# A one-core decoder trunk: six stages a layer with the down projection amid the next stage's gate and up, and 28 groups of seven products in place of 16

## The chip, the cores and the metric

One core of a Trainium2 chip runs the whole program. The metric is the device time of one execution in microseconds (us).

## The reference

Two layers over 256 tokens of 2048 features. The first mixes tokens with a causal pooling, the second with latent attention; each then has the same feed-forward part, which is what the change touches:

```python
def swiglu(h, w_gate, w_up, w_down):
    return (jax.nn.silu(h @ w_gate) * (h @ w_up)) @ w_down

x = x + swiglu(rms_norm(x, ffn_norm[l]), w_gate[l], w_up[l], w_down[l])   # for each of the two layers
```

`w_gate` and `w_up` are 2048 x 5632, `w_down` is 5632 x 2048, all float32.

## The kernel before

**Numbers.** Every float32 factor is split in two rounded parts, hi and lo, and a product is three matmuls: hi x hi, hi x lo, lo x hi. Weights stream from memory into `raw` in chunks of 128 x 1024 elements. ScalarE writes `w_hi` (its `split`), VectorE writes `w_lo = raw - w_hi` (its `split`), into one of four slots (`SPLIT_SLOTS`). TensorE reads both. Chunk n + 4 can be split only when TensorE has ended chunk n (`chunks_used`), and TensorE starts a chunk when its lo part is there (`lo_ready`).

**Plain chunks.** The 5632 features of the hidden layer are 44 tiles of 128. For a plain tile four chunks (two of gate, two of up, half of the 2048 inputs each) are each eight pairs of matmuls: `w_hi` against hi and lo of the activations side by side (512 columns), `w_lo` against hi (256 columns), L634 and L635.

**Groups of seven products.** Two tiles at a time can be computed by a scheme of Strassen's kind: the inputs (two halves) and the tokens (two halves) make a 2 x 2 block product, done with seven half-size products P1 to P7 in place of eight. Each product is two chunks of four times three matmuls of 256 columns (L804, L806, L807). The four weight quarters W11, W12, W22, W21 lie in eight slots of `raw`. Some products need sums of quarters, made in place: first `W11 += W12` (for P5), then `W11 += W22` (P6), `W12 += W22` (P7), `W21 += W11` (P4). The first two are VectorE's (`add_quarter`, L1674), the last two are DMAs that accumulate within SBUF, issued by GpSimd (L2214). The products go P1, P5, P6, P2, P7, P3, P4. They add up in PSUM, and between them intermediate sums are copied out: ScalarE's `part_copy` (L1239) takes P1, then P5, then P1 + P6; TensorE's P2 waits for the copy of P5, P7 for that of P6 (`part_copied`). VectorE adds, gates and multiplies (L1712, L1718), and TensorE turns four blocks back with transposes (L819).

**Order.** A layer's 44 tiles go in three passes of 16, 14 and 14 tiles, with 2, 3 and 3 groups. `up_order` mixes each pass's group chunks evenly with its plain chunks, with plain chunks alone at the head and seven at the end. After a pass's gate and up comes its down projection, 16 output tiles of 14 or 16 products each from two chunks, added into the residual `x` by VectorE (`into_x`, L1791, L1792). Each engine runs its own instruction list in order. Loads are issued by SyncE in an order worked out from when slots come free (`up_loads`): plain chunks have three slots of their own, a quarter's slot is reloaded once its last product is split, and W11's once the fourth sum has landed.

Of the kernel before, what the change touches and what calls it, by code (L numbers as in the profile page):

```python
# [44 lines left out]
P = 128  # L45
# [29 lines left out]
PLAIN_SLOTS = 3  # L75
# [31 lines left out]
PRODUCTS = ("P1", "P5", "P6", "P2", "P7", "P3", "P4")  # L107
# [4 lines left out]
def up_order(q):  # L112

    groups = PASS_GROUPS[q]
    seven = [("S", g, r, c) for g in range(groups) for r in PRODUCTS for c in range(2)]
    plain = [("P", p, c) for p in range(PASS_TILES[q] - 2 * groups) for c in range(4)]
    lead, tail = PASS_LEAD[q], PASS_TAIL
    order, mixed, done = plain[:lead], plain[lead:len(plain) - tail], 0
    for k, s in enumerate(seven):
        order.append(s)  # L120
        upto = (k + 1) * len(mixed) // len(seven)
        order += mixed[done:upto]
        done = upto
    return order + plain[len(plain) - tail:]


UP_ORDER = [up_order(q) for q in range(PASSES)]
PLAIN_TILES = [t - 2 * g for t, g in zip(PASS_TILES, PASS_GROUPS)]
PLAIN_BEFORE = [sum(PLAIN_TILES[:q]) for q in range(PASSES + 1)]
GROUPS_BEFORE = [sum(PASS_GROUPS[:q]) for q in range(PASSES + 1)]  # L130
UPS = [f"up{q}" for q in range(PASSES)]
DOWNS = [f"down{q}" for q in range(PASSES)]
# [23 lines left out]
def up_pass(n):  # L156

    for q in range(PASSES):
        if CHUNK[UPS[q]] <= n < CHUNK[DOWNS[q]]:
            return q  # L160
    return None


def up_step(n):

    q = up_pass(n)
    return None if q is None else UP_ORDER[q][n - CHUNK[UPS[q]]]


PLAIN_AT = [CHUNK[UPS[q]] + k for q in range(PASSES) for k, s in enumerate(UP_ORDER[q]) if s[0] == "P"]  # L170
PLAIN_NO = {n: k for k, n in enumerate(PLAIN_AT)}
GROUP_AT = {(GROUPS_BEFORE[q] + s[1], s[2], s[3]): CHUNK[UPS[q]] + k
            for q in range(PASSES) for k, s in enumerate(UP_ORDER[q]) if s[0] == "S"}


def raw_slot(n):
# [4 lines left out]
    if s[0] == "P":  # L181
        return RING_SLOTS + PLAIN_NO[n] % PLAIN_SLOTS
# [8 lines left out]
def freed_by(g, w, c):  # L191

    return GROUP_AT[g, {"W11": "P2", "W12": "P7", "W22": "P3", "W21": "P4"}[w], c]
# [7 lines left out]
def up_loads(q):  # L201

    loads = []
    for k, s in enumerate(UP_ORDER[q]):
        n = CHUNK[UPS[q]] + k
        if s[0] == "P":
            before = PLAIN_NO[n] - PLAIN_SLOTS
            free = PLAIN_AT[before] if before >= 0 else 0
            loads.append((max(free, CHUNK[UPS[q]] - 1), n, ("chunk", n)))
    for g in range(GROUPS_BEFORE[q], GROUPS_BEFORE[q + 1]):  # L210
        for w in QUARTERS:
            for c in range(2):
                free = freed_by(g - 1, w, c) + (3 if w == "W11" else 0) if g > GROUPS_BEFORE[q] else 0
                if free == 0 and q % LAYER_PASSES == 0 and w in ("W22", "W21"):
                    free = CHUNK[UPS[q]] + MIX_STEPS + SPLIT_SLOTS
                loads.append((max(free, wanted_by(g, w, c) - 14, CHUNK[UPS[q]] - 1), wanted_by(g, w, c),
                              ("quarter", g, w, c)))
# [3 lines left out]
UP_LOADS = [up_loads(q) for q in range(PASSES)]  # L221


def load_numbers():

    numbers, count, order = {}, [0] * (RING_SLOTS + PLAIN_SLOTS), []
    for n in range(CHUNK["end"]):
        q = up_pass(n)
        if q is None:
            order.append(("chunk", n))  # L230
        elif n == CHUNK[UPS[q]]:
            order += UP_LOADS[q]
# [39 lines left out]
def trunk(nc, xT, positions, consts, bands, gains, pool_first, pool_w, w_kv_a, w_k_pe, w_q_a, w_kv_k, w_kv_v, w_q_nope, w_q_pe,  # L272
          w_o, w_plain, w_group, w_down_first, w_down_rest, w_last, final_gain, out):
    with ExitStack() as ctx:
# [8 lines left out]
        raw = sb("raw", [P, RING_SLOTS + PLAIN_SLOTS, TILES * P])  # L283
# [31 lines left out]
        act = at("act", [P, max(PASS_TILES), 2 * SEQ], F32R, region_at + 32 * KB)  # L315
# [33 lines left out]
        angle, turns = part[:, 0, :], part[:, 1, :]  # L349
# [40 lines left out]
        landed = [sem(f"landed{s}") for s in range(RING_SLOTS + PLAIN_SLOTS)]  # L390
# [1993 lines left out]
```

## Time and profile before

| | us |
|---|---|
| median of 3 runs | 1746.03 (1745.45 to 1746.16) |
| the profiled execution, its own time | 1746.25 |
| its span, first to last instruction | 1744.4 |
| TensorE busy | 1736.1 |
| VectorE busy | 1339.1 |
| ScalarE busy | 986.0 |
| GpSimd busy | 168.2 |

The profile is of one execution. The span leaves out 1.85 us of the execution's own time. An engine's busy time is the time in which at least one of its instructions ran; TensorE's matmuls overlap, so a mean duration of one is longer than the time from one to the next.

### The profile page before, as it was taken

The numbers are of one execution on the slowest core, as the hardware profiler recorded it, in microseconds if no ns is written. First come the engines' busy times: TensorE is split into PE (matmuls) and PEld (weight loads), VectorE is DVE, ScalarE is ACT, GpSimd is POOL, SyncE is SP. The second block draws the span as 40 slices with busy tenths as digits, with TensorE's granted clock in tenths as the row PEclk, the third lists the DMA queues.
The fourth block names the chain that finished last, engine by engine and source line by source line (L and its number), as shares of the span: only waits on it lengthen the run. The fifth ranks groups of instructions, "written<-read, shape, count | busy, mean of one in ns | idle before, by whom it ended". The sixth has DMA issues, their size and how long they took to land. (4 is left out here: it accounts for less than half of the span.)

```text
span 1744.4 us, 29460 instructions
## 1 busy us (share of the span) xinstructions
PE 1736.1 (100%) x11142; PEld 1575.2 (90%) x11142; DVE 1339.1 (77%) x1772; ACT 986.0 (57%) x1336; POOL 168.2 (10%) x196
## 2 busy tenths in 40 slices
PE   9999999999999999999999999999999999999998
PEld 6899988999889999889999888998899998899987
DVE  5898766788667886788997779876678866788665
ACT  6666543566435665466775456664356653466543
POOL 2100000000000000324112420000000000000000
PEclk9999999999999999999999999999999999999999
DMA  6678665786767876665445457867568866688762
GB/s 227 216 231 245 234 192 190 238 252 170 248 200 203 251 232 216 200 199 159 150 139 170 156 165 244 242 186 252 196 191 246 247 214 203 200 252 243 227 214 91
DMA packets 103937, 363.24 MB, mean 208 GB/s; under 512 B 11664, under 2 KB 13072, under 8 KB 103696
## 3 DMA queue, kind: packets, MB, share of 16 engines
q1 hardware_dynamic: 94320, 327.03, 54.5%
q0 software_dynamic: 9216, 33.56, 11.2%
q8 instruction: 74, 1.21, 0.3%
q10 hardware_dynamic: 288, 1.11, 0.2%
q14 instruction: 39, 0.32, 0.1%
HBM read 326.01 MB, written 2.10 MB: 188 GB/s over the span
## 5 line engine op out<-in xcount | busy, mean ns | idle before, releaser
L1594 DVE TENSOR_TENSOR w_lo<-raw,w_hi 128x1024 fp32r<-128x1024 f32 (+1 forms) x720 | 858.0, 1201 | 257.3 <-ACT w_hi L1148 251.4
L1148 ACT ACTIVATE w_hi<-raw 128x1024 fp32r<-128x1024 f32 (+1 forms) x721 | 741.4, 1035 | 473.9 <-PE ps L635 390.2
L634 PE MATMUL ps<-xg,w_hi 128*128 128x512 f32 x1856 | 653.2, 392 | 0.8 <-DVE w_lo L1594 0.3
L635 PE MATMUL ps<-xg,w_lo 128*128 128x256 f32 x1856 | 522.9, 282 | 0.0
L634 PE MATMUL ps<-act,w_hi 128*128 128x512 f32 x1352 | 469.2, 390 | 0.0
L634 PEld LDWEIGHTS ps<-xg,w_hi 128*128 128x128 f32 x1856 | 348.4, 188 | 72.2 <-DVE w_lo L1594 2.3
L635 PE MATMUL ps<-act,w_lo 128*128 128x256 f32 x1352 | 381.2, 282 | 0.0
L635 PEld LDWEIGHTS ps<-xg,w_lo 128*128 128x128 f32 x1856 | 350.4, 189 | 0.0
L634 PEld LDWEIGHTS ps<-act,w_hi 128*128 128x128 f32 x1352 | 253.8, 188 | 53.1
L635 PEld LDWEIGHTS ps<-act,w_lo 128*128 128x128 f32 x1352 | 255.5, 189 | 0.0
L2214 POOL DMA_DIRECT2D raw<-raw x64 | 55.3, 865 | 1128.5 <-DVE raw L1674 977.6
L806 PE MATMUL ps<-w_lo,mix_hi_lo 128*128 128x256 f32 x512 | 144.1, 281 | 0.0
L807 PE MATMUL ps<-w_hi,mix_hi_lo 128*128 128x256 f32 x512 | 143.7, 281 | 0.0
L804 PE MATMUL ps<-w_hi,mix_hi_lo 128*128 128x256 f32 x512 | 143.7, 281 | 0.0
L806 PE MATMUL ps<-w_lo,xg 128*128 128x256 f32 x384 | 108.1, 282 | 0.0
L804 PE MATMUL ps<-w_hi,xg 128*128 128x256 f32 x384 | 107.9, 281 | 0.0
L807 PE MATMUL ps<-w_hi,xg 128*128 128x256 f32 x384 | 107.8, 281 | 0.0
L804 PEld LDWEIGHTS ps<-w_hi,mix_hi_lo 128*128 128x128 f32 x512 | 96.4, 188 | 2.7
L807 PEld LDWEIGHTS ps<-w_hi,mix_hi_lo 128*128 128x128 f32 x512 | 96.5, 189 | 0.0
L806 PEld LDWEIGHTS ps<-w_lo,mix_hi_lo 128*128 128x128 f32 x512 | 96.4, 188 | 0.0
L634 PE MATMUL ps<-heads,w_hi 128*128 128x512 f32 x256 | 89.1, 391 | 0.0
L1674 DVE TENSOR_TENSOR raw<-raw 128x1024 f32<-128x1024 f32 x64 | 78.0, 1219 | 0.0
(232 smaller groups left out, 1961.8 us busy)
## 6 DMA issues: line engine op xcount, KB each, us to landing
raw<-w_plain SPq DMA_DIRECT2D x224, 512.0 KB, 4.6
raw<-w_group SPq DMA_DIRECT2D x128, 512.0 KB, 5.8
raw<-w_down_rest SPq DMA_DIRECT2D x120, 448.0 KB, 4.1
raw<-raw POOLq DMA_DIRECT2D x64, 512.0 KB, 5.7
raw<-w_down_first SPq DMA_DIRECT2D x64, 512.0 KB, 4.4
raw<-w_o SPq DMA_DIRECT2D x32, 512.0 KB, 3.5
raw<-w_q_a SPq DMA_DIRECT2D x8, 512.0 KB, 4.2
raw<-w_kv_a SPq DMA_DIRECT2D x8, 512.0 KB, 4.3
```

Source lines behind the costliest of these rows:

```text
L634: pe.matmul(ps[:, bank, :], w_hi[:, s, j * P:(j + 1) * P], moving, start=start, stop=False)
L635: return pe.matmul(ps[:, bank, 0:SEQ], w_lo[:, s, j * P:(j + 1) * P], moving[:, 0:SEQ], start=False, stop=stop)
L804: pe.matmul(dst, x_hi, wh, start=(kt == 0 and r in ("P1", "P5")), stop=False, skip_group_check=True)
L806: pe.matmul(dst, x_hi, wl, start=False, stop=False, skip_group_check=True)
L807: mm = pe.matmul(dst, x_lo, wh, start=False, stop=(kt == TILES - 1), skip_group_check=True)
L1148: nc.scalar.activation(dst, src, ACT.Copy).then_inc(hi_ready, 1)
L1594: nc.vector.tensor_tensor(lo, src, hi.bitcast(F32), ALU.subtract).then_inc(lo_ready, 1)
L1674: nc.vector.tensor_tensor(raw[:, dst, :], raw[:, dst, :], raw[:, src, :], ALU.add).then_inc(done, 1)
L2214: gp.dma_start(raw[:, quarter_slot(into, c), :], raw[:, quarter_slot(of, c), :], accum_op=ALU.add).then_inc(done, 16)
```

## The change

A layer now has one up list, `UP_ORDER`, of 340 chunks for six stages of 8, 6, 6, 8, 8, 8 tiles with 0, 3, 2, 3, 3, 3 groups: 14 groups a layer, 28 in all, and 16 plain tiles a layer. The down projection of a stage is 16 chunks (D), one for each output tile, of 6 or 8 pairs of matmuls, mixed between the next stage's group and plain chunks; only the last stage's down comes by itself at the end. The D chunks share the plain chunks' three slots. Down results are added to `x` after each D chunk (`down_out_of`). The products go P1, P5, P2, P6, P7, P3, P4. The second sum, `W11 += W22`, is an accumulating DMA too, so GpSimd issues six a group where it issued four. Two of the buffers `part` are doubled by `square` and `root`. The table of angles for the rotary phases is made by VectorE in steps amid the first layer's list.

```diff
-PASSES = 6
-LAYER_PASSES = PASSES // 2
-PASS_TILES = (16, 14, 14, 16, 14, 14)
-PASS_GROUPS = (2, 3, 3, 2, 3, 3)
-PASS_LEAD = (24, 4, 4, 24, 4, 4)
-PASS_TAIL = 7
+LAYERS = 2
+STAGE_TILES = (8, 6, 6, 8, 8, 8)
+STAGE_GROUPS = (0, 3, 2, 3, 3, 3)
+STAGES = len(STAGE_TILES)
+STAGE_PLAIN = tuple(t - 2 * g for t, g in zip(STAGE_TILES, STAGE_GROUPS))
+LAYER_GROUPS, LAYER_PLAIN = sum(STAGE_GROUPS), sum(STAGE_PLAIN)
+HALF = max(STAGE_TILES)
 MIX_STEPS = 18
-FH = PASS_TILES[-1]
+GROUPS_FROM = 20
+SETTLE = 8
+ROPE_AT = tuple(range(40, 92, 4))
+TURN_AFTER = 6
+TAIL = 8
+W11_LAG = 5
+FH = STAGE_TILES[-1]
...
-PRODUCTS = ("P1", "P5", "P6", "P2", "P7", "P3", "P4")
+PRODUCTS = ("P1", "P5", "P2", "P6", "P7", "P3", "P4")
...
+    seven = [[("S", sum(STAGE_GROUPS[:s]) + g, r, c) for g in range(STAGE_GROUPS[s]) for r in PRODUCTS for c in range(2)]
+             for s in range(STAGES)]
+    plain = [[("P", sum(STAGE_PLAIN[:s]) + p, c) for p in range(STAGE_PLAIN[s]) for c in range(4)] for s in range(STAGES)]
+    early = plain[0][GROUPS_FROM:]
+    order = plain[0][:GROUPS_FROM] + evenly(early, seven[1][:len(early)])
+    seven[1] = seven[1][len(early):]
+    for s in range(1, STAGES):
+        down = [("D", s - 1, d) for d in range(DT)]
+        last = plain[s][-TAIL:] if s == STAGES - 1 else []
+        rest = plain[s][:len(plain[s]) - len(last)]
+        first = min(len(rest), SETTLE // 3)
+        order += evenly(seven[s][:SETTLE - first], rest[:first])
+        order += evenly(seven[s][SETTLE - first:], evenly(down, rest[first:])) + last
+    return order
+
+
+UP_ORDER = up_order()
+UPS = [f"up{layer}" for layer in range(LAYERS)]
...
-    return GROUP_AT[g, {"W11": "P2", "W12": "P7", "W22": "P3", "W21": "P4"}[w], c]
+    return GROUP_AT[g, {"W11": "P6", "W12": "P7", "W22": "P3", "W21": "P4"}[w], c]
...
+        def part_of(g, at):
+
+            if g % 2 and at in (0, 2):
+                return (square if at == 0 else root)[:, :]
+            return part[:, at, :]
...
+            def down_chunk(layer, k):
+
+                _, s, d = UP_ORDER[k]
+                n, before = CHUNK[UPS[layer]] + k, downs_before(layer, k)
+                pe.wait_ge(lo_ready, made(n))
+                if d == 0:
+                    pe.wait_ge(group_ready, layer * LAYER_GROUPS + sum(STAGE_GROUPS[:s + 1]))
+                    pe.wait_ge(act_ready, layer * LAYER_PLAIN + sum(STAGE_PLAIN[:s + 1]))
+                if before >= 2:
+                    pe.wait_ge(down_out, before - 1)
+                for j in range(STAGE_TILES[s]):
+                    mm = product3(n, j, down_bank(layer, before), act[:, act_slot(s, j), :], j == 0, j == STAGE_TILES[s] - 1)
+                mm.then_inc(chunks_used, 1)
+
...
+                turned_before = g if at == 1 else g - 1
+                if turned_before >= 1:
+                    sc.wait_ge(part_turned, turned_before)
+                nc.scalar.activation(part_of(g, at), src, ACT.Copy).then_inc(part_copied, 1)
...
-                elif step[2] == "P5":
-                    add_quarter(g, "W22", step[3], second_sum)
...
+            def down_out_of(layer, k, d):
+
+                bank, xd = down_bank(layer, downs_before(layer, k)), x[:, d, :]
+                ve.wait_ge(chunks_used, done_at(layer, k))
+                step(nc.vector.tensor_tensor(xd, ps[:, bank, 0:SEQ], xd, ALU.add))
+                nc.vector.tensor_tensor(xd, ps[:, bank, SEQ:], xd, ALU.add).then_inc(down_out, 1)
...
-                        gp.wait_ge(second_sum, 2 * g + c + 1)
+                        gp.wait_ge(landed[quarter_slot("W22", c)], 16 * LOAD_NO["quarter", g, "W22", c])
+                        gp.wait_ge(lo_ready, made(GROUP_AT[g, "P5", c]))
+                        add_quarter("W11", "W22", c, second_sum[c])
+                    for c in range(2):
                         add_quarter("W12", "W22", c, third_sum[c])
                     for c in range(2):
-                        gp.wait_ge(lo_ready, made(GROUP_AT[g, "P2", c]))
+                        gp.wait_ge(lo_ready, made(GROUP_AT[g, "P6", c]))
                         add_quarter("W21", "W11", c, fourth_sum[c])
```

TensorE, in the second group of the first layer's list, before. These are the last matmuls of a plain chunk (L634, L635) and the first three of P2, which waits for the copy of P5:

```order
L634 MATMUL ps<-xg,w_hi 128x512
L635 MATMUL ps<-xg,w_lo 128x256
L804 MATMUL ps<-w_hi,xg 128x256 [waits part_copied,lo_ready]
L806 MATMUL ps<-w_lo,xg 128x256
L807 MATMUL ps<-w_hi,xg 128x256
```

Between P5 and this row stand both chunks of P6 and plain chunks. TensorE, the change, in the fourth group (number 3): the last matmuls of P5's second chunk (L895 to L898, inputs `mix_hi_lo`) and the first of P2 (inputs `xg`):

```order
L895 MATMUL ps<-w_hi,mix_hi_lo 128x256
L897 MATMUL ps<-w_lo,mix_hi_lo 128x256
L898 MATMUL ps<-w_hi,mix_hi_lo 128x256
L895 MATMUL ps<-w_hi,xg 128x256 [waits part_copied,lo_ready]
L897 MATMUL ps<-w_lo,xg 128x256
L898 MATMUL ps<-w_hi,xg 128x256
```

P2, with its wait for the copy, now stands right behind P5. So it is in nine of the layer's 14 groups; in the other five a D or plain chunk is between. P7 stands right behind P6, whose copy it waits for, in four groups (6, 9, 11 and 12), where before P2's two chunks were between.

ScalarE, before, in the second group: the copies (L1239) and the hi splits (L1148) around them, from the first split that needs the second sum on:

```order
L1148 ACTIVATE w_hi<-raw 128x1024 [waits chunks_used,second_sum]
L1148 ACTIVATE w_hi<-raw 128x1024 [waits chunks_used,landed9]
L1148 ACTIVATE w_hi<-raw 128x1024 [waits chunks_used,second_sum]
L1239 ACTIVATE part<-ps 128x256 [waits part_turned,chunks_used]
L1148 ACTIVATE w_hi<-raw 128x1024 [waits chunks_used,landed10]
```

ScalarE, the change, in the second group (number 1, `square` and `root` are its copies' buffers), around the copies of P1 and P5:

```order
L1330 ACTIVATE square<-ps 128x256 [waits chunks_used]
L1238 ACTIVATE w_hi<-raw 128x1024 [waits chunks_used,landed7]
L1238 ACTIVATE w_hi<-raw 128x1024 [waits chunks_used,second_sum0]
L1330 ACTIVATE root<-ps 128x256 [waits chunks_used]
L1238 ACTIVATE w_hi<-raw 128x1024 [waits chunks_used,second_sum1]
```

The split of P6's first chunk, which waits for the second sum's DMA (`second_sum0`), stands ahead of the copy of P5 (the row on `root`). So it is in groups 1 and 11 of each layer, where ten and eleven group chunks follow one another with no D or plain chunk between; in the other groups the copy comes first.

On GpSimd's list the third sums are now issued right behind the second ones (the last lines of the diff), so four accumulating DMAs of a group stand one behind the other in its queue, and two more follow once P6's chunks are split.

## Rows read from the trace of the kernel before

**Rows 1.** The page: span, busy time by engine; DMA queues: packets, MB, share

```profile
span 1744.4 us, 29460 instructions
...
PE 1736.1 (100%) x11142; PEld 1575.2 (90%) x11142; DVE 1339.1 (77%) x1772; ACT 986.0 (57%) x1336; POOL 168.2 (10%) x196
...
q1 hardware_dynamic: 94320, 327.03, 54.5%
q0 software_dynamic: 9216, 33.56, 11.2%
```

**Rows 2.** Groups by line and form: xcount | busy us, mean ns | idle before

```profile
L1148 ACT ACTIVATE w_hi<-raw 128x1024 fp32r<-128x1024 f32 x593 | 624.2, 1058 | 358.6 <-PE ps L635 275.1 <-DMA raw<-w_plain 41.6 <-PE ps L807 32.4
...
L1674 DVE TENSOR_TENSOR raw<-raw 128x1024 f32<-128x1024 f32 x64 | 78.0, 1219 | 0.0
```

**Rows 3.** The chain of waits, of TensorE's weight loads: total us, times, longest

```profile
PEld ps L634 <- DVE w_lo L1594: 2.3, 7, 0.5
```

**Rows 4.** Timeline, TensorE: start us, us; a plain chunk, two group chunks, the next

```profile
372.07 0.39 PE L634 MATMUL ps<-xg,w_hi 128*128 128x512 f32 x1
...
374.86 0.28 PE L804 MATMUL ps<-w_hi,xg 128*128 128x256 f32 x1
...
377.70 0.39 PE L634 MATMUL ps<-xg,w_hi 128*128 128x512 f32 x1
```

**Rows 5.** Timeline, TensorE: eight pairs in a stretch of plain chunks

```profile
79.65 0.39 PE L634 MATMUL ps<-xg,w_hi 128*128 128x512 f32 x1
...
82.42 0.39 PE L634 MATMUL ps<-xg,w_hi 128*128 128x512 f32 x1
```

**Rows 6.** Timeline, TensorE: the four transposes of a group

```profile
156.91 0.60 PE L819 MATMUL ps<-const,part 128*128 128x128 f32 x4
157.27 0.37 PE L804 MATMUL ps<-w_hi,xg 128*128 128x256 f32 x1
157.47 0.28 PE L806 MATMUL ps<-w_lo,xg 128*128 128x256 f32 x1
```

**Rows 7.** Timeline, all engines: a group product ends, ScalarE copies it

```profile
118.51 0.28 PE L807 MATMUL ps<-w_hi,mix_hi_lo 128*128 128x256 f32 x1
118.83 0.39 ACT L1239 ACTIVATE part<-ps 128x256 f32<-128x256 f32 x1 [0.15 <-PE ps L807]
...
118.90 0.51 PE L634 MATMUL ps<-xg,w_hi 128*128 128x512 f32 x1
...
119.24 0.28 PE L635 MATMUL ps<-xg,w_lo 128*128 128x256 f32 x1
```

**Rows 8.** Timeline, ScalarE, then VectorE: end of an up stretch, last plain tile

```profile
218.16 0.60 ACT L1224 ACTIVATE cross<-ps 128x512 f32<-128x512 f32 x1 [1.65 <-PE ps L635]
...
221.22 0.42 ACT L1232 ACTIVATE act<-product 128x256 fp32r<-128x256 f32 x1 [0.49 <-DVE product L1700]
...
221.67 0.42 DVE L1705 TENSOR_TENSOR act<-product,act 128x256 fp32r<-128x256 f32 x1 [0.48 <-ACT act L1232]
```

**Rows 9.** The accumulating DMAs' line: their issue on GpSimd, their landing

```profile
L2214 POOL DMA_DIRECT2D raw<-raw x64: 852/862/1010, 115.4 to 1613.8; - x64
...
DMA to landing us min/median/max: 4.5/5.7/9.4
```

**Rows 10.** Timeline, VectorE: a down tile's two adds between two splits

```profile
481.63 0.42 DVE L1791 TENSOR_TENSOR x<-ps,x 128x256 f32 x1 [0.47 <-PE ps L635]
...
482.50 1.09 DVE L1594 TENSOR_TENSOR w_lo<-raw,w_hi 128x896 fp32r<-128x896 f32 x1
```

**Rows 11.** Timeline, VectorE: four splits one after the other

```profile
164.10 4.63 DVE L1594 TENSOR_TENSOR w_lo<-raw,w_hi 128x1024 fp32r<-128x1024 f32 x4
```

**Rows 12.** Windows of 10 us: PE, PEld, DVE, ACT, POOL busy, clock, DMA share, GB/s

```profile
360.00:370.00 10.00, 10.00 (x72) 9.35 (x71) 9.96 (x12) 6.97 (x12) 1.72 (x2) 1.00 0.82 191
610.00:620.00 10.00, 10.00 (x72) 9.34 (x71) 8.91 (x14) 6.71 (x9) 0.00 (x0) 1.00 1.03 411
160.00:170.00 10.00, 10.00 (x71) 9.35 (x71) 8.78 (x10) 7.23 (x10) 1.72 (x2) 1.00 1.00 226
```

More of the change, by code:

```diff
@@ L127, with evenly @@
[L127 to L132, printed above, removed]
+def evenly(a, b):
+    out, done = [], 0
+    for k, item in enumerate(a):
+        out.append(item)
+        upto = (k + 1) * len(b) // len(a)
+        out += b[done:upto]
+        done = upto
+    return out
@@ L135, in chunk_plan, with stage_of, plain_tile, group_tile @@
+UP_ORDER = up_order()
+UPS = [f"up{layer}" for layer in range(LAYERS)]
+DOWNS = [f"down{layer}" for layer in range(LAYERS)]
+def stage_of(before, k):
+    return next(s for s in range(STAGES) if k < sum(before[:s + 1]))
+def plain_tile(p):
+    s = stage_of(STAGE_PLAIN, p)
+    return s, 2 * STAGE_GROUPS[s] + p - sum(STAGE_PLAIN[:s])
+def group_tile(g):
+    s = stage_of(STAGE_GROUPS, g)
+    return s, 2 * (g - sum(STAGE_GROUPS[:s]))
+def act_slot(s, f):
+    return s % 2 * HALF + f
 def chunk_plan():
@@ L191, in freed_by, with up_loads @@
 def freed_by(g, w, c):
-    return GROUP_AT[g, {"W11": "P2", "W12": "P7", "W22": "P3", "W21": "P4"}[w], c]
+    return GROUP_AT[g, {"W11": "P6", "W12": "P7", "W22": "P3", "W21": "P4"}[w], c]
 def wanted_by(g, w, c):
     return GROUP_AT[g, {"W11": "P1", "W12": "P1", "W22": "P5", "W21": "P2"}[w], c]
[L201 to L210, printed above, removed]
+def up_loads(layer):
+    loads, first = [], CHUNK[UPS[layer]]
+    for k, s in enumerate(UP_ORDER):
+        n = first + k
+        if s[0] != "S":
+            before = STREAM_NO[n] - STREAM_SLOTS
+            free = STREAM_AT[before] if before >= 0 else 0
+            loads.append((max(free, first - 1), n, ("chunk", n)))
+    for g in range(layer * LAYER_GROUPS, (layer + 1) * LAYER_GROUPS):
@@ L211, in up_loads @@
         for w in QUARTERS:
             for c in range(2):
[L213 to L217, printed above, removed]
+                if g > layer * LAYER_GROUPS:
+                    free = freed_by(g - 1, w, c) + (W11_LAG if w == "W11" else 0)
+                elif w in ("W22", "W21"):
+                    free = first + MIX_STEPS + SPLIT_SLOTS
+                else:
+                    free = first - 1
@@ L218, in up_loads @@
+                loads.append((max(free, wanted_by(g, w, c) - 14, first - 1), wanted_by(g, w, c), ("quarter", g, w, c)))
     return [load for _, _, load in sorted(loads, key=lambda x: x[:2])]
-UP_LOADS = [up_loads(q) for q in range(PASSES)]
+UP_LOADS = [up_loads(layer) for layer in range(LAYERS)]
 def load_numbers():
-    numbers, count, order = {}, [0] * (RING_SLOTS + PLAIN_SLOTS), []
+    numbers, count, order = {}, [0] * (RING_SLOTS + STREAM_SLOTS), []
     for n in range(CHUNK["end"]):
-        q = up_pass(n)
-        if q is None:
+        layer = up_layer(n)
+        if layer is None:
@@ L1862, in _ @@
+                n1, t1 = CHUNK[DOWNS[layer]], TILE[DOWNS[layer]]
+                for d in range(DT):
+                    into_x(t1 + d, d, n1 + d + 1)
+                    split(n1 + d + SPLIT_SLOTS)
+                    gained(d, G_ATTN, xg, xg_before + d + 1)
+            ffn(0, 2, DT)
             xk_tiles = iter(range(DT))
```

690 lines of the change are left out of this document (341 added, 349 removed).

## Prediction

> **What bounds the kernel now.** I read the page first. TensorE is busy for 1736.1 of a span of 1744.4 us, VectorE for 1339.1, ScalarE for 986.0 [rows 1]; so TensorE is the bound unless its busy time hides waits. The chain of waits says that it hides hardly any: for a split chunk TensorE waited 2.3 us in all, in seven waits of at most 0.5 [rows 3]. A timeline of TensorE then gives the price of its work. The start of one chunk to the start of the next is 2.79 us for a plain chunk and, over two, 1.42 us for a group chunk [rows 4]; where only plain chunks run, eight pairs take 2.77 [rows 5]. The kernel's time is therefore the sum of these pieces. The windows say how near the others are: between 360 and 370 us VectorE is busy for 9.96 of 10 us while TensorE still never stands, and the DMA share touches 1.00 with and without accumulating DMAs [rows 12].
>
> **What TensorE gains.** Two tiles as plain chunks are 8 x 2.78 (between the two rows) = 22.2 us; as a group 14 x 1.42 = 19.9 us [rows 4, 5]: 2.36 us less. Twelve more groups give 28.3. Each also brings four transposes: from 156.91 to 157.27, and the matmul behind them holds 0.20 where 0.12 is usual, 0.44 us in all [rows 6], 12 times 5.3. Net **-23.0** (-22.1 to -24.0 with the one or the other price of a plain chunk). The down projection has as many pairs as before but for the last quarter of the last layer, where 24 pairs more (8.3 us) stand against six fewer inputs of the closing part: three matmuls of 512 and six of 256 columns each, about 1.4 us apiece, 8.4. I count that as nothing.
>
> **What the new product order costs.** This is the term on which the sign hangs. P2 waits for ScalarE's copy of P5, and P7 for that of P6. Before, at least two group chunks (2.84 us) lay between; now none does in 9 + 4 of a layer's 14 groups, 26 places in all. What such a place costs is seen in a product that ends and is copied: its last matmul starts at 118.51, the copy at 118.83, 0.32 later, and takes 0.39 [rows 7]. From one engine's end to the next one's start is 0.03 (ScalarE's 221.22 + 0.42 to VectorE's 221.67) [rows 8]. TensorE's next matmul would have started 0.12 after the last; so it starts 0.32 + 0.39 + 0.03 - 0.12 = 0.62 late. The first matmul after a stand also holds longer: 118.90 to 119.24, 0.34, against 2.77 / 8 - 0.12 = 0.23 [rows 5, 7]. That is 0.11 more, with rounding 0.74 a place, 26 times **+19.2**. From below: without the last 0.11 and the tail of the copy I would still have 0.48 (12.5 in all). From above: ScalarE may still hold a split (1.06 us [rows 2]) or a gate when the product ends, at most half a microsecond more, 1.2 a place, 31 in all. I take 0.74, since ScalarE is free in rows 7.
>
> **The end of a layer's up list.** Before, the last plain tile was the 14th or 16th input of the first down tile. From the copy of its cross terms to its finished lo part are 221.67 + 0.42 - 218.16 = 3.93 us [rows 8]; 13 pairs at 0.346 are 4.5, so nothing stood. Now it is the eighth input, reached after 7 x 0.346 = 2.42 us. With 0.32 ahead and 0.03 and 0.11 behind, less the 0.12, TensorE stands 0.32 + 3.93 + 0.14 - 2.54 = 1.85 us, in both layers **+3.7** (bounds 3 and 5).
>
> **The second sum as a DMA.** An accumulating DMA lands 5.7 us (4.5 to 9.4) after its issue [rows 9], where VectorE's sum took 1.22 [rows 2]. P6's split can begin only then. The lo part of a chunk is there some 2.6 us after TensorE ends the chunk four ahead: ScalarE's 1.06, VectorE's 1.22 [rows 2] and hops; the DMA of P5's first chunk thus lands at 2.6 + 5.7 = 8.3 from that end. In 12 groups of a layer TensorE has 11 us and more of work up to the ScalarE step that needs it. In groups 1 and 11 it is different, and here the order rows on ScalarE count: the split of P6 stands ahead of the copy of P5, so P2 can start only at 8.3 + 1.06 + 0.39 + 0.1 = 9.9. TensorE gets to P2 in group 1 after five group chunks, 7.1 us, and in group 11 after a plain chunk and four group chunks, 8.45. It stands 2.8 and 1.45, of which 0.74 each is counted above: 2.1 and 0.7 more. In group 11 a second wait follows. Four DMAs stand behind one another, and the last must have landed for P7's second chunk. The accumulating queue took 11.2% of the span for 64 DMAs, 3.05 us each [rows 1]; the last lands near 2.6 + 2 + 4 x 3 = 16.6, and with the split's 2.3 the chunk is ready at 18.9. TensorE is there at 9.9 + 4 x 1.42 + 0.74 + 1.42 = 17.7: 1.2 less rounding, say 0.7. Together 3.5 a layer, **+7.0**. From below: with the shortest landing (4.5) and the loads aside, 4, and nothing if TensorE comes later than I think. From above: with 9.4 in place of 5.7 the two groups lose 3.7 more each, and then the reload of W11, which waits for the fourth sum, is late too: 24 in all.
>
> Here a page would give another sum. The Trainium skill ("DMA: Bandwidth & Descriptors", section "Anatomy of one DMA — SWDGE (gpsimd) path") puts a GpSimd-issued DMA at 2.0 us plus its bytes at 436 GB/s; by that, 512 KB would land in 3.2 us, both waits would all but vanish and my sum would be 7 us lower, 1746. The trace disagrees, 4.5 us at least [rows 9], so I keep the row.
>
> **What should stay hidden.** DMA throughput: a load at full share runs at 411 GB/s, 1.28 us for 512 KB, while with accumulating DMAs in the mix the same full share moves 226 GB/s [rows 12]. A stage with three groups has 48 loads (61 us) and 18 sums (55 us), 116 us under TensorE's 42 x 1.42 + 24 x 2.78 = 126: 92%. It fits on average; if not, it is rival A. VectorE in such a stage: 66 splits at (4.63 - 1.22) / 3 = 1.14 us [rows 11] are 75, six first sums 7, sixteen down tiles at 0.87 [rows 10] 14, gates and plain tiles 12: 108 of 126. It gives up the second sums and takes twice as many down adds. Its cover is the distance of four chunks, and rows 12 show it full for 10 us without a stand of TensorE; were that cover gone, each us over would count in full. GpSimd issues 104 DMAs more at 0.86 us [rows 9], and it has nothing else in these stretches.
>
> **Sum.** -23.0 + 19.2 + 3.7 + 7.0 = +6.9 us. The profiled execution took 1746.25, its span and 1.85; the median of the runs is 1746.03, so no correction is due. 1746.25 + 6.9 = **1753**.
>
> **Rivals.** Less than 0.2% (3.5 us) can't be told from no change here.
> A, the DMA engines become the bound. For it: 92% as an average, a full share in several windows, and four sums in a row that slow the loads. Against it: loads run ahead. With landings of 9.4 us throughout, the DMA term is 24 in place of 7: 1770 (from 1760 on I call it this case). Chance 0.2.
> B, on the other side: the copies cost TensorE nothing, because it can take up P2's matmuls before P5's copy is through (the ends of matmuls are modelled, so the 0.32 may be partly a matter of record). Then -23.0 + 3.7 + 7.0 = -12.3: 1734. It becomes faster by 0.2% once a place costs less than (23.0 - 10.7 - 3.5) / 26 = 0.34 us. Against it: the wait is on TensorE's own list, and 0.48 is my lower bound. Chance 0.2, since pieces of the other terms may help it.
> C, no change: a place costs 0.48, the rest stands: -23.0 + 12.5 + 10.7 = +0.2, 1746. Chance 0.18.
> My forecast, a loss of 3.5 to 14 us: 0.42.
>
> **The numbers.** Slower has the forecast and A, 0.62; same 0.18; faster 0.2. The forecast's own range is 1750 to 1760. The range for 8 in 10 cuts half of B and the far part of A: 1738 to 1771.
>
> **What would show it.** In the profile after, TensorE's idle time should stand on the copy's line, 26 waits of about 0.6 us on ScalarE's copy, 18 ahead of P2 and 8 ahead of P7. TensorE's busy time should fall by some 20 us and its idle time rise by some 30. Each layer should show a stand of about 1.8 us in the first down tile of the last stage, and some 3 us at each of groups 1 and 11 behind a DMA. The forecast is wrong if TensorE stands for splits in many places (then VectorE or the DMAs bound it), or if P2's first matmul follows P5's last within 0.4 us. The DMA share should rise from 0.66 over the span to near 0.85.

## The result and the profile after

The changed kernel takes **1781.12 us** (1779.15 to 1782.52, 4 runs), the kernel before, beside it on the same chip, 1745.74 (1745.38 to 1746.16): ratio **1.0202**, 95% interval 1.0187 to 1.0217. The forecast was 1753, with a range up to 1771. The sign was right and the size far off: 35 us were lost and not 7.

The page of the kernel after, its first lines, queues and a few of its groups (line, engine, tiles, count, busy us, mean ns, idle time before):

```profile
span 1779.7 us, 30241 instructions
...
PE 1731.3 (97%) x11664; PEld 1591.3 (89%) x11664; DVE 1467.7 (82%) x2029; ACT 1068.1 (60%) x1433; POOL 272.7 (15%) x300
...
q1 hardware_dynamic: 94464, 327.03, 50.7%
q0 software_dynamic: 24192, 88.09, 26.9%
...
L703 PE MATMUL ps<-act,w_hi 128*128 128x512 f32 x1376 | 486.6, 392 | 3.1 <-DVE act L1792 3.1
L703 PE MATMUL ps<-xg,w_hi 128*128 128x512 f32 x1088 | 384.0, 393 | 3.5 <-DVE w_lo L1674 3.5
...
L895 PE MATMUL ps<-w_hi,mix_hi_lo 128*128 128x256 f32 x896 | 255.4, 285 | 14.6 <-ACT part L1330 12.3
...
L895 PE MATMUL ps<-w_hi,xg 128*128 128x256 f32 x672 | 192.0, 286 | 19.3 <-ACT root L1330 12.6
```

Span less busy time was 8.3 us on TensorE [rows 1]; it is 48.4 now. The accumulating queue (q0) went from 11.2% to 26.9%. The chain of waits after, TensorE's rows (line and tile, what was waited for: us in total, times, longest):

```profile
PE ps L895 <- ACT part L1330: 15.7, 15, 4.8
PE ps L895 <- ACT root L1330: 12.6, 8, 3.5
PE ps L895 <- DVE w_lo L1674: 5.6, 8, 1.3
PE ps L703 <- DVE w_lo L1674: 3.5, 9, 0.6
PE ps L703 <- DVE act L1792: 3.1, 2, 1.5
```

Where [rows 3] had 2.3 us, ScalarE's copies (L1330, into part, or square and root in odd groups) now hold TensorE for 28.3 us in 23 waits. By TensorE's own starts all 26 places where P2 or P7 stands right behind P5 or P6 have a stand; at four of them the profile names a low split instead, and one of the 23 waits is at no such place. The stands are of two kinds. The first is the kind that was foreseen, here ahead of P2 in group 2, all engines; it answers to [rows 7]:

```profile
211.23 0.28 PE L898 MATMUL ps<-w_hi,mix_hi_lo 128*128 128x256 f32 x1
...
211.55 0.38 ACT L1330 ACTIVATE part<-ps 128x256 f32<-128x256 f32 x1 [0.29 <-PE ps L898]
...
212.08 0.36 PE L895 MATMUL ps<-w_hi,xg 128*128 128x256 f32 x1 [0.56 <-ACT part L1330]
```

P5's last matmul starts at 211.23, its copy 0.32 later, P2 at 212.08 where 211.35 was due: a stand of 0.72 to 0.73 us, which 20 of the 26 places show to the hundredth. P2's first matmul then holds 0.20 us where 0.12 is usual, so that a place costs 0.80 us. The other six lie in groups 1 and 11. The timeline of group 1:

```profile
155.98 1.22 DVE L1764 TENSOR_TENSOR raw<-raw 128x1024 f32<-128x1024 f32 x1
...
157.85 1.22 DVE L1674 TENSOR_TENSOR w_lo<-raw,w_hi 128x1024 fp32r<-128x1024 f32 x1
...
159.12 0.39 PE L895 MATMUL ps<-w_hi,mix_hi_lo 128*128 128x256 f32 x1 [1.31 <-DVE w_lo L1674]
...
159.60 0.86 POOL L2299 DMA_DIRECT2D raw<-raw  x1 [29.90 <-DVE w_lo L1674]
...
161.95 0.28 PE L898 MATMUL ps<-w_hi,mix_hi_lo 128*128 128x256 f32 x1
...
164.26 1.06 ACT L1238 ACTIVATE w_hi<-raw 128x1024 fp32r<-128x1024 f32 x1 [3.80 <-DMA raw<-raw]
165.23 0.36 ACT L1330 ACTIVATE root<-ps 128x256 f32<-128x256 f32 x1
...
165.74 0.55 PE L895 MATMUL ps<-w_hi,xg 128*128 128x256 f32 x1 [3.51 <-ACT root L1330]
...
166.30 0.42 PE L898 MATMUL ps<-w_hi,xg 128*128 128x256 f32 x1
166.52 0.41 PE L895 MATMUL ps<-w_hi,xg 128*128 128x256 f32 x1
```

Three things are to be seen. P5's low split (157.85) is ready only when TensorE already stands for it (159.12); the cover of four chunks is gone, because VectorE has had its first sums (155.98) among the splits of neighbouring chunks, and 1.4 us of gates, additions into `part` and the angle table besides (layer 1, which makes no table, stands 1.1 us there where this layer stands 1.5). The second sum is therefore issued only at 159.60. ScalarE stands 3.80 us for its landing, to split P6's first chunk, and P5's copy is queued behind that split; P2 needs only the copy, and starts at 165.74 where 162.07 was due. And from one matmul to the next it is then 0.22 us, not 0.12: TensorE has come out of the stand at half clock. Group 11 has the same ahead of P2 and a longer one ahead of P7 (GpSimd, ScalarE, TensorE):

```profile
600.92 2.63 POOL L2299 DMA_DIRECT2D raw<-raw  x3 [1.86 <-DVE w_lo L1674]
...
611.08 1.06 ACT L1238 ACTIVATE w_hi<-raw 128x1024 fp32r<-128x1024 f32 x1 [1.45 <-DMA raw<-raw]
...
612.33 1.04 ACT L1238 ACTIVATE w_hi<-raw 128x1024 fp32r<-128x1024 f32 x1
613.28 0.36 ACT L1330 ACTIVATE part<-ps 128x256 f32<-128x256 f32 x1
...
613.78 0.36 PE L895 MATMUL ps<-w_hi,mix_hi_lo 128*128 128x256 f32 x1 [3.62 <-ACT part L1330]
```

P6's copy (613.28) stands behind the split of P7's second chunk (611.08), which waits for the last of three sums issued together, and behind P3's first. Windows over two of these places (us, busy time of PE, PEld, DVE, ACT, POOL, granted clock, DMA share, GB/s), and the sums' landings over the span:

```profile
160.00:180.00 20.00, 16.49 (x107) 15.82 (x107) 13.94 (x19) 10.26 (x13) 4.82 (x6) 0.83 1.00 204
...
1600.00:1620.00 20.00, 16.77 (x107) 16.14 (x108) 15.07 (x20) 11.66 (x15) 0.00 (x0) 0.83 0.93 303
...
DMA to landing us min/median/max: 4.5/8.7/17.9
```

A clock of 0.83 is a mean: 6.8 of the 20 us were granted at 1.2 GHz and the rest at 2.4. In both up lists together 20.5 us are at 1.2 GHz, in four stretches that each begin in the last 2 us of a long stand of group 1 or 11, or within 1.3 us behind it; before, the clock left 2.4 GHz only in the last microseconds.

From the starts of all matmuls, with waits above 0.25 us counted and the 1.5 us of the kernel before taken off, the account is:

| term | predicted us | after |
|---|---|---|
| TensorE's work (744 pairs less at 0.347, 672 triples more at 0.355, closing part -8.4, 48 transposes more, 5.7) | -23.0 | -22.3 |
| copies in 20 places (0.72 stood, 0.08 in the slow first step) | 14.8 | 16.0 |
| groups 1 and 11 (the DMA term 7.0 and six copies 4.4) | 11.4 | 23.7 |
| ends of the up lists | 3.7 | 3.4 |
| other waits, for splits | 0 | 4.1 |
| half clock (by e8 below) | 0 | 8.5 |
| sum | 6.9 | 33.4 |

The span grew by 35.3; the other 2 us are waits too short to be listed and a longer half-clock end (6.4 us where 3.2 were), and were not divided.

### The profile page after: what moved, and what is told of

It reads as the page before. It is cut to its first block, busy times and chain, and to the rows that moved or that the text cites. A ratio compares the mean times of both kernels' runs of the same rounds, so it can differ in the third digit from the quotient of the medians.

```text
span 1779.7 us, 30241 instructions
## 1 busy us (share of the span) xinstructions
PE 1731.3 (97%) x11664; PEld 1591.3 (89%) x11664; DVE 1467.7 (82%) x2029; ACT 1068.1 (60%) x1433; POOL 272.7 (15%) x300
## 3 DMA queue, kind: packets, MB, share of 16 engines
q0 software_dynamic: 24192, 88.09, 26.9%
q10 hardware_dynamic: 288, 1.11, 0.2%
## 4 chain that ended last, share of the span: by engine, by line
PE 84%; DVE 9%; DMA 3%; ACT 2%; issue 1%; POOL 0%; SPq 0%; DVEq 0%; ACTq 0%; POOLq 0%
PE ps L703 31%; PE ps L704 16%; PE ps L895 9%; PE ps L898 9%; PE ps L897 9%; DVE w_lo L1674 4%; DMA raw<-raw 2%; PE ps L777 1%; ACT w_hi L1238 1%; PE ps L711 1%; DVE raw L1764 1%; PE ps L712 1%; PE ps L713 1%; DMA raw<-w_stream 1%; DVE sums L1783 1%
## 5 line engine op out<-in xcount | busy, mean ns | idle before, releaser
L1674 DVE TENSOR_TENSOR w_lo<-raw,w_hi 128x1024 fp32r<-128x1024 f32 (+2 forms) x793 | 945.3, 1200 | 217.2 <-ACT w_hi L1238 214.1
L1238 ACT ACTIVATE w_hi<-raw 128x1024 fp32r<-128x1024 f32 (+2 forms) x794 | 820.2, 1036 | 491.7 <-PE ps L704 332.2
L703 PE MATMUL ps<-xg,w_hi 128*128 128x512 f32 x1088 | 384.0, 393 | 3.5 <-DVE w_lo L1674 3.5
L704 PE MATMUL ps<-xg,w_lo 128*128 128x256 f32 x1088 | 306.4, 282 | 0.0
L895 PE MATMUL ps<-w_hi,mix_hi_lo 128*128 128x256 f32 x896 | 255.4, 285 | 14.6 <-ACT part L1330 12.3
L898 PE MATMUL ps<-w_hi,mix_hi_lo 128*128 128x256 f32 x896 | 253.7, 283 | 0.0
L703 PEld LDWEIGHTS ps<-xg,w_hi 128*128 128x128 f32 x1088 | 204.3, 188 | 47.3 <-DVE w_lo L1674 6.6
L895 PE MATMUL ps<-w_hi,xg 128*128 128x256 f32 x672 | 192.0, 286 | 19.3 <-ACT root L1330 12.6
L704 PEld LDWEIGHTS ps<-xg,w_lo 128*128 128x128 f32 x1088 | 205.4, 189 | 0.0
L898 PE MATMUL ps<-w_hi,xg 128*128 128x256 f32 x672 | 190.5, 283 | 0.0
L895 PEld LDWEIGHTS ps<-w_hi,mix_hi_lo 128*128 128x128 f32 x896 | 170.3, 190 | 21.8 <-DVE w_lo L1674 12.9
L898 PEld LDWEIGHTS ps<-w_hi,mix_hi_lo 128*128 128x128 f32 x896 | 170.5, 190 | 0.0
L895 PEld LDWEIGHTS ps<-w_hi,xg 128*128 128x128 f32 x672 | 128.0, 191 | 26.4 <-issue 17.7
L897 PEld LDWEIGHTS ps<-w_lo,xg 128*128 128x128 f32 x672 | 128.2, 191 | 0.0
```

The costliest lines, as they stand in the source:

```text
L703: pe.matmul(ps[:, bank, :], w_hi[:, s, j * P:(j + 1) * P], moving, start=start, stop=False)
L704: return pe.matmul(ps[:, bank, 0:SEQ], w_lo[:, s, j * P:(j + 1) * P], moving[:, 0:SEQ], start=False, stop=stop)
L895: pe.matmul(dst, x_hi, wh, start=(kt == 0 and r in ("P1", "P5")), stop=False, skip_group_check=True)
L897: pe.matmul(dst, x_hi, wl, start=False, stop=False, skip_group_check=True)
L898: mm = pe.matmul(dst, x_lo, wh, start=False, stop=(kt == TILES - 1), skip_group_check=True)
L1238: nc.scalar.activation(dst, src, ACT.Copy).then_inc(hi_ready, 1)
```

## The experiments

Each was timed against the kernel before beside it. Short names: "order" is the new product order, "sum" the second sum.

**e1, the sum back on VectorE.** Order, stages and groups stay.

```diff
-                        sc.wait_ge(second_sum[c], 16 * (g + 1))
+                        sc.wait_ge(second_sum, 2 * g + c + 1)
...
                     add_quarter(g, "W12", step[3], first_sum)
+                elif step[2] == "P5":
+                    add_quarter(g, "W22", step[3], second_sum)
```

> The changed kernel with its second sum on VectorE again (an addition behind the low split of each P5 chunk, as before the change); stages, 28 groups and new product order stay. Theory W (the excess is waits: 20 copy waits of 0.72 us, two stands a layer behind accumulating DMAs in groups 1 and 11, and the half clock that follows those stands): the stands of groups 1 and 11 shrink to copy waits, no stretch at 1.2 GHz is left inside the two up lists, and the time is 1722 (1745 less 23) + 23 copy or so places x 0.72 + 3.4 at the ends of the lists + some 4 of small ones = 1746 to 1750. Rival V (VectorE is the bound once it carries 56 more additions of 1.22 us): 1760 or more, with lo splits late all over. Rival K (the clock falls whatever the sums do): two to four stretches at 1.2 GHz stay, and the time is 1755 to 1760.

Measured 1773.5 us, ratio 1.0155 (1.0138 to 1.0172): only 8 us less than the change, and above what theory W gave. Half clock came once a layer. The timeline of VectorE in group 1 says why the sums' place matters so little there:

```profile
158.51 1.22 DVE L1674 TENSOR_TENSOR w_lo<-raw,w_hi 128x1024 fp32r<-128x1024 f32 x1
159.64 1.22 DVE L1764 TENSOR_TENSOR raw<-raw 128x1024 f32<-128x1024 f32 x1
160.78 0.34 DVE L1808 SCALAR_TENSOR_TENSOR part<-part,row_rstd 128x128 f32<-128x128 f32 x1
161.04 1.22 DVE L1674 TENSOR_TENSOR w_lo<-raw,w_hi 128x1024 fp32r<-128x1024 f32 x1
162.18 1.22 DVE L1764 TENSOR_TENSOR raw<-raw 128x1024 f32<-128x1024 f32 x1
```

Split to split is 2.53 us (158.51 to 161.04) for a chunk that TensorE does in 1.42. Where P1's and P5's chunks have no stream chunk (a plain or a D chunk) between them, TensorE falls to that pace: it stands 1.11 us a chunk. So my first theory, in which the DMA alone was at fault in groups 1 and 11, fell.

**e2, the old order as well; what is left of the change is stages and 28 groups.** **e3, the old order with the sum as DMA.**

```diff
-PRODUCTS = ("P1", "P5", "P2", "P6", "P7", "P3", "P4")
+PRODUCTS = ("P1", "P5", "P6", "P2", "P7", "P3", "P4")
-    return GROUP_AT[g, {"W11": "P6", "W12": "P7", "W22": "P3", "W21": "P4"}[w], c]
+    return GROUP_AT[g, {"W11": "P2", "W12": "P7", "W22": "P3", "W21": "P4"}[w], c]
```

> The changed kernel with the old product order (P1, P5, P6, P2, P7, P3, P4) and the second sum on VectorE: what is left of the change is the stages with their down chunks and the 28 groups alone. Theory W: no copy is waited for, so 1722 + 3.4 at the ends + some 4 = 1728 to 1732, clearly faster than before. Rival G (the gain of 23 us from twelve more groups isn't there, or the one list costs it again): 1740 to 1750.

> The changed kernel with only the old product order; the second sum stays an accumulating DMA, so its landing now has two chunks of products less to hide behind. Theory W (a sum's landing of 6 to 9 us sets what follows it): TensorE stands at P6 in most groups, 1755 to 1790, with the stands at P6 c0 in place of P2 c0. Rival C (the DMA is not what hurts, the copies behind neighbours are): about as e2, 1728 to 1738.

e2 took 1754.4 (1.0046, 1.0029 to 1.0063), e3 1835.1 (1.0509, 1.0492 to 1.0527). Rows of their chains of waits, first e2's:

```profile
PE ps L703 <- DVE w_lo L1674: 10.3, 14, 1.6
PE ps L895 <- DVE w_lo L1674: 9.4, 12, 1.3
PE ps L703 <- DVE act L1794: 3.1, 2, 1.5
```

And e3's:

```profile
PE ps L895 <- DVE w_lo L1674: 62.9, 31, 4.4
```

With the sum on VectorE the order costs 1773.5 - 1754.4 = 19.1. e3 says what it is for: in the old order P6 comes two chunks sooner, and TensorE stands for its split in nearly every group. e3 lies 45 us above theory W's range; it has ten stretches at 1.2 GHz, 41 us in all, of which its expectation says nothing. e2 was 22 us above its expectation. The gain in work is there, but the waits for splits go against it: 19.7 us by the profile, 24 by TensorE's starts. The stages with their 28 groups alone lose already.

**e4, the places apart.** Where P2 follows P5 or P7 follows P6, the next stream chunk is moved between.

```diff
+    for k in range(len(order) - 4):
+        a, b = order[k:k + 2]
+        if a[0] == b[0] == "S" and a[1] == b[1] and (a[2], b[2]) in (("P5", "P2"), ("P6", "P7")):
+            for j in range(k + 2, k + 5):
+                if order[j][0] != "S":
+                    order.insert(k + 1, order.pop(j))
+                    break
```

> The changed kernel with one more rule for the list: where P2 stands right behind P5, or P7 right behind P6, the next stream chunk is moved between them (20 of 24 places; groups 1 and 11 keep theirs, having no stream chunk near). Theory W: the 20 waits of 0.72 us go and nothing else moves, 1780 less 14 = 1764 to 1768, the half clock in groups 1 and 11 stays. Rival M (the waits only hide another lateness, of splits or landings, which shows once they go): 1775 or more.

1760.2 (1.0080, 1.0063 to 1.0097), 21 less than the change and 4 below theory W's range. It was 22 of 26 places that got a chunk between, not 20 of 24. The 20 waits of 0.72 are gone, and the stand ahead of P7 in group 11 with one of its half-clock stretches too, as the rule finds a chunk there after all. One stretch a layer stays, behind group 1.

**e5, the runs broken up; e6, both; e7, e2 broken up; e11, e6 with the sum on VectorE.** The edit that e5 adds:

```diff
-TAIL = 8
+TAIL = 6
...
-        order += evenly(seven[s][:SETTLE - first], rest[:first])
-        order += evenly(seven[s][SETTLE - first:], evenly(down, rest[first:])) + last
+        settle = SETTLE if s > 1 else 4
+        order += evenly(seven[s][:settle - first], rest[:first])
+        order += evenly(seven[s][settle - first:], evenly(down, rest[first:])) + last
```

> The changed kernel (1781) with the two runs of group chunks in a row broken up: the down chunks of stage 1 begin after 4 group chunks and not 8, and two plain chunks of the last stage stand among the products of group 11 (tail 6 and not 8). Order and accumulating DMAs stay; 12 places a layer have P2 behind P5 or P7 behind P6. Theory Z (those two runs are where VectorE and the sums' DMAs fall behind, and the half clock follows the stands there): stands of groups 1 and 11 fall from some 12 us a layer to 2, no stretch at 1.2 GHz stays inside the lists, 1781 less 8 less 8 less 11 = 1750 to 1758. Rival P (the sums' landings of 8.7 us are too long wherever they stand, and the stands just move to other groups): 1768 or more.

> As e5, and a stream chunk between every P5 and P2 and every P6 and P7, so no copy is waited for. Theory Z: e5 less 24 x 0.72 = 17, that is 1733 to 1741, faster than the kernel before (1746.5). Rival P: 1750 or more.

> As e2 (old product order, second sum on VectorE, 1754.4) with the runs broken up as in e5. Theory Z (in e2 the stands are VectorE, which needs 2.5 us for each of P1's and P5's chunks where they stand in a row and TensorE 1.4): of the 27 us of stands in e2 the 14 of groups 1, 11 and 12 go, 1740 to 1744. Rival L (VectorE is short over the whole list, at 87% busy, and what is saved there stands elsewhere): 1750 or more.

> e6 (1740.5) with its second sum on VectorE again. Theory V (where landings have room, the DMA sum gains what VectorE is then short of): as e7, 1748 to 1752, some 10 slower than e6. Rival A (the DMA engines' extra 27% is a burden of its own, and e6 would be faster without it): 1735 to 1740.

e5 took 1762.7 (1.0104, 1.0085 to 1.0122), e6 **1740.5** (0.9968, 0.9954 to 0.9982), e7 1750.4 (1.0027, 1.0017 to 1.0037), e11 1750.7 (1.0031, 1.0019 to 1.0043). None is at half clock inside the lists in the execution that was profiled. e5's other executions are not all like it: 1759.9 and 1760.3 us came at mean clocks of 0.999 and 1.000, 1765.1 and 1767.3 at 0.998 and 0.996, so its median of 1762.7 lies between two kinds. e6 beats the kernel before; its windows and landings:

```profile
160.00:180.00 20.00, 20.00 (x141) 18.69 (x140) 17.36 (x25) 11.64 (x15) 4.46 (x6) 1.00 1.02 240
...
1600.00:1620.00 20.00, 20.00 (x149) 19.00 (x148) 16.87 (x24) 12.42 (x14) 1.72 (x2) 1.00 1.05 288
...
DMA to landing us min/median/max: 4.6/9.2/16.6
```

Same DMAs, same full DMA share, landings even longer (9.2), and in these windows TensorE never stands: neither the engines' throughput nor the landing as such was the trouble. What is left is what is queued near it, which e13 tests. Over e6's lists TensorE's stands above 0.25 us still add up to 15 us (1.7 before), the longest 1.5, half of them for splits; so of the 22 us of work saved only 5 are seen. e5 missed its range by 5 us, by 2 in the executions at full clock: group 1 kept 1.9 and 2.1 us ahead of P7, and group 11 1.4 and 1.9. e7 missed too: with both sums on VectorE group 1 kept some 4 us of stands, and groups 5 and 8 from 1.3 to 1.7 ahead of a plain chunk, in each layer; so rival L holds in part, VectorE's lateness is not only in the two runs. And e6 against e11 prices the sum as DMA where it has room: it **gains** 10 us.

**e8, TensorE kept going.** In each layer 34 matmuls that nobody reads, into a free bank, ahead of its four long waits.

```diff
+                count = {(1, "P5", 0): 4, (1, "P2", 0): 12, (11, "P2", 0): 6, (11, "P7", 0): 12}.get((number, r, c), 0)
...
+                for _ in range(count):
+                    pe.matmul(ps[:, bank, :], mix_hi_lo[:, 0, 0, 0, :], xg[:, 0, :], start=True, stop=True)
```

> The changed kernel (1781), in which TensorE does products that nobody reads (128x512, 0.23 us each) into a free bank ahead of the four waits that were long: 4 ahead of P5 and 12 ahead of P2 in group 1, 6 ahead of P2 and 12 ahead of P7 in group 11, in each layer, 15 us in all, laid into stands of 22 us. Theory K (the stretches at 1.2 GHz come of TensorE's standing and cost some 10 us by themselves): no stretch at half clock stays inside the lists and the time falls by 6 to 10, to 1771 to 1775. Rival H (the clock falls for another reason, or the fall only fills time that TensorE would have stood anyway): 1779 to 1790.

1772.6 (1.0153, 1.0136 to 1.0170), 8.5 us less than the change for more work. Group 1 in the timeline of TensorE, and a window:

```profile
161.43 2.89 PE L866 MATMUL ps<-xg,mix_hi_lo 128*128 128x512 f32 x12
...
165.10 0.36 PE L907 MATMUL ps<-w_hi,xg 128*128 128x256 f32 x1 [0.78 <-ACT root L1342]
...
160.00:180.00 20.00, 19.22 (x137) 17.77 (x136) 15.49 (x22) 10.77 (x14) 4.36 (x5) 1.00 1.03 217
```

P2 starts nearly as late as before (165.10), the clock stays at 2.4 GHz, and what follows runs at full pace. Theory K holds: the stretches came of standing and cost 8.5 us by themselves. (Two of the three executions that were not profiled read a mean clock of 0.998 and not 1.000, so the price may be a little more.)

**e9 and e10, more from e6.** e9 puts one down chunk between the last two plain tiles of a list and one behind the last; e10 also starts stage 1's down chunks after one group chunk.

```diff
+    order.insert(len(order) - 4, kept[0])
+    order.append(kept[1])
...
-        settle = SETTLE if s > 1 else 4
+        settle = SETTLE if s > 1 else 1
```

> e6 (1740.5) with the last two down chunks of stage 4 taken out of the run of groups: one stands between the last two plain tiles of a layer's list and one behind the last, so that the last plain tile's activation has a chunk of 2.8 us more before stage 5's down tiles ask for it. Theory T (1.7 us a layer at the end of the list is the wait for that activation, as the prediction's term of 3.7 has it): 1740.5 less 3.4 = 1736 to 1738.5. Rival U (two stream chunks fewer among the groups let splits come late there, and eat it): 1739 to 1743.

> e9 with the down chunks of stage 1 begun one group chunk after group 0's last plain chunks and not four, so that a stream chunk stands between P1's two chunks and between P5's in group 1. Theory V (TensorE's 2.3 and 1.9 us there are VectorE's two additions behind neighbouring chunks, 2.4 us of VectorE to 1.4 of TensorE): 3 us less than e9, 1732.5 to 1735.5. Rival D (the first down chunk then waits for group 0's or plain tile 7's activation): e9 or more.

e9 1740.75 (0.9971, 0.9959 to 0.9982), e10 1739.7 (0.9963, 0.9949 to 0.9977): no difference from e6 that can be told. In e9 the stand at the end of a list is gone, which shows that it was the wait for the last activation, but group 12 now waits for splits (0.6 us in each layer, 1.35 more in one): rival U. In e10, e9's 3.9 us in group 1 become 2.7, in one wait a layer ahead of the first down chunk, for a plain tile's activation: the splits come in time once a stream chunk stands between P1's two and P5's two, as theory V has it, and rival D's wait takes their place. Of its waits:

```profile
PE ps L715 <- DVE w_lo L1686: 3.9, 10, 0.6
PE ps L715 <- DVE act L1804: 2.4, 2, 1.3
```

**e12, order and sum alone in the kernel before.** Its passes and 16 groups stay; order, sum and the table of what frees a quarter change as in the diff of the change.

> The kernel before (passes, 16 groups, 1746) with the new product order and the second sum by accumulating DMA, nothing else of the change. Two places a layer have P2 behind P5 or P7 behind P6, and the groups have about as many plain chunks between them as group chunks. Theory Z (order and landings cost only where group chunks stand in a row): 4 x 0.72 = 2.9 more, 1745 to 1751. Rival P (a landing of 8 us hurts in any list): 1756 or more.

1748.9 (1.0016, 1.0007 to 1.0026), 2.9 more: the same two edits that fill the table above cost little in a list where groups and plain chunks alternate. That it is 4 x 0.72 to the tenth is luck: by TensorE's starts two of the places stood 0.7 us and two 1.8, 5.0 in all, and the 1.7 us of small stands of before are gone. Its landings, and its one wait of note:

```profile
DMA to landing us min/median/max: 4.6/9.1/14.6
...
PE ps L804 <- ACT part L1239: 4.3, 4, 1.6
```

**e13, only the copies moved.** Left open so far: spreading takes away both the late landings and what is queued behind them. Here list, order and DMAs are those of the change, and ScalarE makes P5's copy one chunk sooner in its program in groups 1 and 11, P6's two chunks sooner in group 11.

```diff
-                        g = ended(layer, at, "P5")
-                        if g is not None:
-                            part_copy(layer, at, g, 2, ps[:, PAIR, 0:WIDE])
+                        for ahead in (0, 1):
+                            g = ended(layer, at + ahead, "P5")
+                            if g is not None and (g % LAYER_GROUPS in (1, 11)) == (ahead == 1):
+                                part_copy(layer, at + ahead, g, 2, ps[:, PAIR, 0:WIDE])
```

> The changed kernel (1781) with three of ScalarE's copies a layer moved ahead of high splits in its program: P5's copy in groups 1 and 11 by one chunk (ahead of the split of P6's first chunk, which waits for the second sum), P6's copy in group 11 by two (ahead of the splits of P7's second chunk, which waits for the third sum, and of P3's first). Theory S (the long stands ahead of P2 and P7 there are copies that are queued behind a split that waits for a landing; TensorE could have gone on): P2 starts 2.7 us sooner in group 1 and some 1.1 in group 11, P7 2.7 sooner in group 11; part of it comes back at P6 and at P7's second chunk, whose landings are late themselves; with less or no half clock the time is 1763 to 1773. Rival L (the landings themselves bind: each us that P2 gains stands at P6): the stands move, the half clock stays, 1776 to 1783.

1769.4 (1.0134, 1.0117 to 1.0151), 11.7 less than the change. ScalarE and TensorE in the timeline, then a row of the waits:

```profile
161.63 0.38 ACT L1330 ACTIVATE root<-ps 128x256 f32<-128x256 f32 x1 [1.79 <-PE ps L898]
163.62 1.06 ACT L1238 ACTIVATE w_hi<-raw 128x1024 fp32r<-128x1024 f32 x1 [1.60 <-DMA raw<-raw]
...
598.93 0.36 PE L895 MATMUL ps<-w_hi,xg 128*128 128x256 f32 x1 [0.25 <-ACT root L1330]
...
PE ps L895 <- DVE w_lo L1676: 14.8, 17, 1.9
```

The copy stands ahead of the split now, P2 waits 0.72 us for it as anywhere else, and no half clock follows. If the clock is worth e8's 8.5 us here too, 3 of the gain are the stands; the rest of what the stands held came back in smaller pieces, as waits for the splits of P6 and P7 (5.6 us in 8 waits became 14.8 in 17). So both theories have their part: the landings do bind, by 1 to 2 us at a time, and the queue made six long stands out of them, behind which the clock fell.

## Why the prediction was wrong

**TensorE's gain, -23.0: right**, -22.3.

**Copies, 0.74 a place: right within a tenth**, 0.80 in 20 places, though both parts were off: the stand is 0.72 and not 0.62, since from the copy's end to P2's start it is 0.15 us (211.93 to 212.08) and not the 0.03 taken from a VectorE row, and the first step is 0.08 longer, not 0.11. Rivals B and C (0 and 0.48) are out: P2's first matmul never came within 0.4 us.

**Ends of the lists, +3.7: right**, 1.69 a layer; e9 shows the cause.

**The second sum as a DMA, +7.0: this is the step that failed**, and with it the clock, below. Groups 1 and 11 with their copies were put at 11.4 us; 23.7 stood. Three parts of it:
- "The lo part of a chunk is there some 2.6 us after TensorE ends the chunk four ahead." In group 1 the chunk four ahead of P5 ended near 152.6, the lo part came at 159.1. That cover of four chunks assumes that VectorE keeps up with 1.42 us chunks. P1's chunks cost it a split and a first sum, 2.4 us each. I had weighed VectorE over a whole stage, 108 of 126 us, and never over the ten group chunks in a row. These stands alone are 2.2 and 1.8 us. The landing that followed was 4.7 us, less than the 5.7 of the sum: not the landing was late but its start.
- For P2 the prediction had seen that P6's split stands ahead of P5's copy. For P7 it looked only at P7's own second chunk (0.7) and not at P6's copy, queued behind two splits, one of which waits for the last of the sums. That was 3.78 and 4.96 us.
- Without its six copies the term is 19.3, inside its own bounds (4 to 24). The waits of W11's reload, from which I had built the upper one, were no part of it. What the term missed, 12.3 us, would by itself have ended at 1765, within the range; the clock's 8.5 us, the 4.1 of small waits and smaller rests took it to 1781 (e8, without the clock's stretches, is at 1772.6, just outside).

**The clock: not in the prediction at all**, 8.5 us (e8). It followed from the step above: the kernels without the long stands have no fall in their traces.

**"What should stay hidden": right for the DMA engines, half wrong for VectorE.** Over the span the two queues' share rose from 0.66 to 0.78 (forecast 0.85). Landings were long, 8.7 us in the median, which is rival A's condition of 9.4 but for a little, and A's 1770 is the nearest number that I gave. Its mechanism is not the one, though: e6 has landings of 9.2, ScalarE waits for them for 63 us there (38 in the change), and TensorE loses no long stand to them. The Trainium skill ("DMA: Bandwidth & Descriptors", section "Anatomy of one DMA — SWDGE (gpsimd) path") would by estimate give 3.2 us for such a transfer; the trace disagrees, more so after the change (8.7 in the median, 4.5 at the least) than before it (5.7 and 4.5). VectorE's 4.1 us of other waits, beside neighbours, were counted at nothing.

**What the profile should show:** stands at all 26 places foreseen, 22 of them put down to the copy; TensorE's busy time fell by 5 and not by 20, mostly because work at half clock counts double in it (in e6, without any, it fell by 16.3); idle time rose by 40, not 30.

What stays open is how the 4.1 us of small waits and the last 2 us divide. Only e10 spreads VectorE's first sums, in group 1 and upon e9; the wait for an activation that came in their place hides what that is worth.

## What to carry to other kernels

Weigh an engine over the densest run of the list, not over a stage. Here 86% on average hid chunks that ask VectorE for 2.4 us and TensorE for 1.42, and a reordering of the same chunks was worth 40 us (the change against e6), more than the 35 that the change itself cost.

When a wait moves onto a DMA, look at what stands behind the waiting instruction in that engine's program, also if it needs nothing of the DMA. In e13 three copies a layer moved by one or two chunks, and 11.7 us came back.

An edit's price belongs to the list it stands in: the same order and sums cost 2.9 us in the old list (e12), and the same DMA sum gains 10 us where the groups are spread (e6 against e11) and loses 8 where they are not (e1 against the change). Of these 8 most is the clock: e1 has 6.8 us at 1.2 GHz in its lists and the change 20.5, which at e8's price is an estimated 5.7.

## What the runs showed of the hardware

TensorE's granted clock went to 1.2 GHz for 3.4 or 6.8 us at a time in the midst of work, when it had stood 2.1 to 5.0 us at one place or was still standing, mostly with shorter stands just ahead (the change, e1, e3, e4). Not each such stand did it: eight of e3's, of 2.2 to 3.1 us, left it at 2.4 GHz, the longest near 494 us. In the traces of e2, e5 to e7 and e9 to e13, with no stand above 2.2 us, it never did, though two executions of e5 that were not profiled read a lower mean clock (0.998, 0.996) and took 5 to 7 us more. Matmuls that nobody reads in the place of the stand (e8) kept it at 2.4 GHz. Over the change's two lists that is 8.5 us behind 23.7 us of stands.

An accumulating DMA from SBUF to SBUF of 512 KB landed after 4.5 or 4.6 us at the least in every run, and after up to 18.2 (e10). Their number does not order the medians: these are 5.5 to 5.7 us with 64 of them (before) and with 112 (e1, e2, e7, e11), where only the third sums, two, stand right behind one another in GpSimd's queue, and 7.3 to 9.4 with 96 (e12) and 168 (the others), where second and third sums, four, do. In e12 four in a row, issued from 324 to 327 us, landed 4.6, 7.6, 9.8 and 14.2 us after their issue. Of the three issued together from 600.92 us, ScalarE could split the first's sum at 605.76 and the last's at 611.08.
